# Block 2's low-rank gate row: both weight halves in one stationary tile, and its second layer in fp32r

## The reference, cut to what matters

```python
n = rms_norm(x, attn_norm_g)
proj = n @ w_in
(g_qkv, g_lr, g_out, nq, kc, vc, ks, vs, kw, vw, ng) = jnp.split(proj, offsets, axis=-1)
...
# gla_mixer: g_lr is 256 x 16, gate_w2 is 16 x 512
log_a = jax.nn.log_sigmoid((gate_lr @ gate_w2 + gate_b).astype(jnp.float32)) / GLA_GATE_TAU
...
# nsa_mixer: ng is 256 x 24
gates = jax.nn.sigmoid(gate_logits.astype(jnp.float32))
```

## Time and profile before

| what | value |
|---|---|
| median of 3 runs | 2610.11 us (2608.5 to 2611.57) |
| the profiled execution | 2613.08 us, span 2611.3 us |
| PE busy | 2594.8 us, 99% of the span |
| DVE, ACT, POOL busy | 43%, 54%, 46% |
| granted clock of PE, mean | 0.998 |
| transfers | 515.84 MB, 198 GB/s on average |

### The profile page before, as it was taken

The page is one execution under the profiler, slowest core; times in us unless marked ns, Lnnn a source line. Parts: engine busy times, 40 slices in busy tenths (PEclk is TensorE's granted clock), DMA queues, the critical chain, the costliest instruction groups (busy, mean ns, idle before and its releaser), DMA issues.

```text
span 2611.3 us, 30136 instructions
## 1 busy us (share of the span) xinstructions
PE 2594.8 (99%) x11856; PEld 2147.6 (82%) x11856; DVE 1130.2 (43%) x1328; ACT 1408.1 (54%) x1727; POOL 1205.6 (46%) x528
## 2 busy tenths in 40 slices
PE   8999999999999999999999999999999999999999
PEld 6888888788888888888888888878888888888887
DVE  5798955434342232323333466446533232322222
ACT  7667645445565555555544574565555555555333
POOL 2687843344444444444444455333344444444443
PEclk9999999999999999999999999999999999999999
DMA  8666654476566666666666644454666666666564
GB/s 299 214 193 202 191 194 164 148 234 210 191 204 205 208 202 209 202 209 202 209 206 213 208 162 161 160 195 139 184 202 201 209 201 209 202 209 202 201 201 145
DMA packets 174588, 515.84 MB, mean 198 GB/s; under 512 B 108027, under 2 KB 111068, under 8 KB 117104
## 3 DMA queue, kind: packets, MB, share of 16 engines
q1 hardware_dynamic: 174016, 513.40, 61.2%
q10 hardware_dynamic: 432, 0.52, 0.1%
HBM read 487.14 MB, written 2.10 MB: 187 GB/s over the span
## 4 chain that ended last, share of the span: by engine, by line
PE 95%; DVE 2%; ACT 1%; POOL 1%; issue 1%; DMA 0%; SPq 0%; ACTq 0%; DVEq 0%; POOLq 0%
PE PB L735 30%; PE PB L739 30%; PE PB L736 30%; DVE WL L2011 1%; ACT WH L1256 1%; POOL WL L2972 1%; PE PB L971 1%; PE PB L815 0%; PE PB L855 0%; PE PB L845 0%; PE PB L933 0%; PE PB L753 0%; PE PB L1088 0%; PE PB L917 0%; PE PB L1031 0%
## 5 line engine op out<-in xcount | busy, mean ns | idle before, releaser
L2972 POOL TENSOR_TENSOR WL<-RAW,WH 128x1024 fp32r<-128x1024 f32 x441 | 1084.4, 2459 | 1388.4 <-ACT WH L1256 1388.2
L1256 ACT ACTIVATE WH<-RAW 128x1024 fp32r<-128x1024 f32 x889 | 939.0, 1057 | 1078.6 <-PE PB L739 1060.2
L2011 DVE TENSOR_TENSOR WL<-RAW,WH 128x1024 fp32r<-128x1024 f32 x448 | 611.1, 1365 | 1391.1 <-ACT WH L1256 1390.9
L735 PE MATMUL PB<-WH,HNH 128*128 128x512 f32 x2464 | 970.8, 394 | 2.8 <-ACT WH L1544 2.1
L739 PE MATMUL PB<-WL,HNH 128*128 128x512 f32 x2464 | 962.0, 390 | 3.5 <-POOL WL L2972 3.4
L736 PE MATMUL PB<-WH,HNL 128*128 128x512 f32 x2464 | 960.6, 390 | 0.0
L739 PEld LDWEIGHTS PB<-WL,HNH 128*128 128x128 f32 x2464 | 463.3, 188 | 104.4 <-POOL WL L2972 6.3
L735 PEld LDWEIGHTS PB<-WH,HNH 128*128 128x128 f32 x2464 | 463.9, 188 | 102.5 <-issue 6.8
L736 PEld LDWEIGHTS PB<-WH,HNL 128*128 128x128 f32 x2464 | 463.7, 188 | 94.7
L735 PE MATMUL PB<-WH,HDH 128*128 128x512 f32 x704 | 273.9, 389 | 0.0
L736 PE MATMUL PB<-WH,HDL 128*128 128x512 f32 x704 | 273.9, 389 | 0.0
(11 more groups left out here) (377 smaller groups left out, 1930.4 us busy)
## 6 DMA issues: line engine op xcount, KB each, us to landing
RAW<-in_w_gu SPq DMA_DIRECT2D x176, 1024.0 KB, 4.8
RAW<-in_w_dn SPq DMA_DIRECT2D x88, 1024.0 KB, 4.8
RAW<-in_w_in_a SPq DMA_DIRECT2D x53, 1024.0 KB, 5.1
RAW<-in_w_in SPq DMA_DIRECT2D x45, 1024.0 KB, 4.8
RAW<-in_w_out SPq DMA_DIRECT2D x32, 1024.0 KB, 4.8
RAW<-in_w_ga SPq DMA_DIRECT2D x24, 1024.0 KB, 4.8
RAW<-in_w_gb SPq DMA_DIRECT2D x24, 1024.0 KB, 4.8
WIN<-in_win SPq DMA_DIRECT2D x8, 512.0 KB, 6.0
```

The source lines that it names most:

```text
L735: e.matmul(o, hi[:, k, x], WH[:, s, c], start=k == 0, stop=False)
L1256: e.activation(WH[:, u % NSPL, :], RAW[:, n % NRAW, half * SU * 128:(half + 1) * SU * 128], ACT.Copy).then_inc(*wt.act.mark(("wh", u)))
L2011: e.tensor_tensor(WL[:, u % NSPL, :], RAW[:, n % NRAW, half * SU * 128:(half + 1) * SU * 128], f32(WH[:, u % NSPL, :]), ALU.subtract).then ...
L2972: e.tensor_tensor(WL[:, u % NSPL, :], RAW[:, n % NRAW, half * SU * 128:(half + 1) * SU * 128], f32(WH[:, u % NSPL, :]), ALU.subtract).then ...
```

## The change

**The row.** The 40 columns are laid out in 64: `g_lr` (16), the first 16 of `ng`, `g_lr` again, the last 8 of `ng` with 8 of zeros; the 64 stand twice in the tile of 128. `WH` gets the rounded weights as before. The subtraction of the row's two units then writes the rest into the second 64 columns of `WH` itself (`low_of`), so that a stationary tile holds the high halves in its first 64 columns and the low halves in the others. Two products, with the high and with the low input, replace three. The wait for the low half stands ahead of a unit's first product.

**The second layer.** `GW2` is loaded as four stacked copies (128 x 512), each 16 rows and 16 of zeros. ACT rounds it to `GWR`, at step 3 of the row; DVE replaces the rows 32 to 47 and 96 to 111 by the low part, two operations at step 10. `LRS` is rounded to `LRH` by ACT (step 4 of `c1`) and its rest goes to `LRL` by DVE (step 7 of `c1`). Eight fp32r products with 128 rows replace four fp32 products with 16.

**The gates.** PE adds up high and low logits and turns them in one step, two fp32 products of `LRS` (stationary) with a table of ones, `gsel`, 24 columns wide, now in `c1` at tile 20. ACT takes the Sigmoid from PSUM at step 27 of `c1`; Sigmoid and copy on `GT` are gone.

```diff
+        def low_of(u):
+
+            n, half = divmod(u, 2)
+            raw, hi = RAW[:, n % NRAW, half * SU * 128:(half + 1) * SU * 128], WH[:, u % NSPL, :]
+            if u // 2 != both_halves // 2:
+                return WL[:, u % NSPL, :], raw, f32(hi)
+            raw, hi = (x.rearrange("p (t s c) -> p t s c", s=2, c=64)[:, :, 1, :] for x in (raw, hi))
+            return hi, raw, f32(hi)
...
                     if r == 0:
-                        e.wait_ge(*wt.act.done("wh", u))
+                        e.wait_ge(*low_half(u))
                     e.matmul(o, WH[:, s, c], hi[:, k, :], start=n == 0, stop=False)
-                    e.matmul(o, WH[:, s, c], lo[:, k, :], start=False, stop=False)
-                    if r == 0:
-                        e.wait_ge(*low_half(u))
-                    t = e.matmul(o, WL[:, s, c], hi[:, k, :], start=False, stop=last)
+                    t = e.matmul(o, WH[:, s, c], lo[:, k, :], start=False, stop=last)
...
             def decay_rows():
                 bz = [wide_bank("z", 0), wide_bank("z", 1)]
-                e.wait_ge(*m.act.done("lr"))
-                e.wait_ge(landed["gw2"], 16)
+                e.wait_ge(*m.act.done("lrh"))
+                e.wait_ge(*m.dve.done("gw"))
+                e.wait_ge(*m.dve.done("lrl"))
                 for h in range(4):
-                    t = e.matmul(bz[h // 2][:, (h % 2) * T:(h % 2 + 1) * T], GW2[:, h * 128:(h + 1) * 128], LR[:, :],
-                                 start=True, stop=True)
+                    z, w2 = bz[h // 2][:, (h % 2) * T:(h % 2 + 1) * T], GWR[:, h * 128:(h + 1) * 128]
+                    e.matmul(z, w2, LRH[:, :], start=True, stop=False)
+                    t = e.matmul(z, w2, LRL[:, :], start=False, stop=True)
...
             for k in tiles(16):
+                if k == 3:
+                    e.wait_ge(landed["gw2"], 16)
+                    e.wait_ge(*m.dve.done("lm"))
+                    e.activation(GWR[:, :], GW2[:, :], ACT.Copy).then_inc(*m.act.mark("gw"))
...
-                if k == 5:
+                if k == 4:
                     e.wait_ge(*m.dve.done("lr"))
-                    e.activation(LR[:, :], LRS[0:16, :], ACT.Copy).then_inc(*m.act.mark("lr"))
-                    e.activation(GT[32:56, :], LRS[32:56, :], ACT.Sigmoid).then_inc(*m.act.mark("gt"))
+                    e.activation(LRH[:, :], LRS[:, :], ACT.Copy).then_inc(*m.act.mark("lrh"))
+                if k == 27:
+                    e.wait_ge(*m.pe.done("gate"))
+                    e.activation(flat(GATE[:, :, :]), bank("gate")[:, 0:48], ACT.Sigmoid).then_inc(
+                        *m.act.mark("gate", frees("gate")))
...
+                if k == 10:
+                    e.wait_ge(*m.act.done("gw"))
+                    for p in (slice(32, 48), slice(96, 112)):
+                        e.tensor_tensor(GWR[p, :], GW2[p, :], f32(GWR[p, :]), ALU.subtract).then_inc(
+                            *m.dve.mark(*(["gw"] if p.start == 96 else [])))
...
+                if k == 7:
+                    e.wait_ge(*m.act.done("lrh"))
+                    e.tensor_tensor(LRL[:, :], LRS[:, :], f32(LRH[:, :]), ALU.subtract).then_inc(*m.dve.mark("lrl"))
```

More of the change, by code:

```diff
@@ L35, in vec_layout @@
                     ("qg", 1), ("kcg", 1), ("ksg", 1), ("kwg", 1),
-                    ("f1", 1), ("b1", 1), ("f2", 1), ("b2", 1), ("gbias", 1), ("gsum", 72)):
+                    ("f1", 1), ("b1", 1), ("f2", 1), ("b2", 1), ("gbias", 1), ("gsum", 72), ("gsel", 24)):
         VECS[name] = (n, k)
@@ L316, in build @@
         RST = ar("RST", [128, T], 47)
-        LR = ar("LR", [16, T], 38)
+        LRH = ar("LRH", [128, T], 38, F32R)
+        LRL = ar("LRL", [128, T], 39, F32R)
         LRS = ar("LRS", [128, T], 64)
-        GW2 = ar("GW2", [16, 512], 36)
+        GW2 = ar("GW2", [128, 512], 36)
+        GWR = ar("GWR", [128, 512], 32, F32R)
         MGH = ar("MGH", [128, 8, T], 48, F32R)
@@ L327, in build @@
         AM = ar("AM", [128, 384], 84)
-        GT = ar("GT", [56, T], 85.5)
         GATE = ar("GATE", [128, 2, 24], 86.5)
@@ L368, in build @@
         units = 2 * len(order)
+        both_halves = 2 * order.index(("w_in2", 4))
         def is_split(u):
@@ L1183, in gates_turned @@
                 bank = wide_bank("gate")
-                e.wait_ge(*m.act.done("gt"))
+                n = VECS["gsel"][0]
+                e.wait_ge(*m.dve.done("lr"))
                 for c in range(2):
-                    t = e.transpose(bank[:, c * 24:(c + 1) * 24], GT[32:56, c * 128:(c + 1) * 128], IDENT[32:56, 32:56])
+                    t = e.matmul(bank[:, c * 24:(c + 1) * 24], LRS[:, c * 128:(c + 1) * 128], VEC[:, n:n + 24],
+                                 start=True, stop=True)
                 t.then_inc(*m.pe.mark("gate"))
@@ L1190, in tensor @@
             tile_row(NT["lr"], 16, None, {2: lambda: scales_in_rows(2, ST), 8: lambda: turn_group("cg", 0)})
-            group(NT["c1"], HNH, HNL, 16, None, {16: decay_rows})
+            group(NT["c1"], HNH, HNL, 16, None, {16: decay_rows, 20: gates_turned})
             w.marks = second_marks(w.i)
@@ L1197, in tensor @@
                     group(NT["og"] + 2 * j, HNH, HNL, 16, None,
-                          {} if j else {8: lambda: turn_group("cg", 1), 32: gates_turned})
+                          {} if j else {8: lambda: turn_group("cg", 1)})
                 elif name == "v":
@@ L2008, in low @@
                     return
-                n, half = divmod(u, 2)
+                to, raw, hi = low_of(u)
                 e.wait_ge(*wt.act.done("wh", u))
-                e.tensor_tensor(WL[:, u % NSPL, :], RAW[:, n % NRAW, half * SU * 128:(half + 1) * SU * 128],
-                                f32(WH[:, u % NSPL, :]), ALU.subtract).then_inc(*wt.dve.mark(("wl", u)))
+                e.tensor_tensor(to, raw, hi, ALU.subtract).then_inc(*wt.dve.mark(("wl", u)))
             def tiles(n):
@@ L2589, in heads @@
                         if h == 0:
-                            e.wait_ge(*m.dve.done("gate"))
+                            e.wait_ge(*m.act.done("gate"))
                         for c in range(2):
@@ L2923, in vector @@
                             conv_earlier("cg", 1, (k - 14) // 4)
[L2924 to L2927, removed]
                     elif name == "v" and j or name == "kc":
@@ L2969, in low @@
                     return
-                n, half = divmod(u, 2)
+                to, raw, hi = low_of(u)
                 e.wait_ge(*wt.act.done("wh", u))
-                e.tensor_tensor(WL[:, u % NSPL, :], RAW[:, n % NRAW, half * SU * 128:(half + 1) * SU * 128],
-                                f32(WH[:, u % NSPL, :]), ALU.subtract).then_inc(*wt.pool.mark(("wl", u)))
+                e.tensor_tensor(to, raw, hi, ALU.subtract).then_inc(*wt.pool.mark(("wl", u)))
             def tiles(n):
@@ L3211 @@
         groups(w[:, 0:512]),
-        units(tiles(padded(np.concatenate([padded(w[:, 2048:2064], 32), w[:, 5648:5672]], axis=1)))),
+        units(tiles(np.concatenate([np.concatenate([w[:, 2048:2064], w[:, 5648:5664], w[:, 2048:2064],
+                                                    padded(w[:, 5664:5672], 16)], axis=1)] * 2, axis=1))),
         groups(w[:, 512:1024]), groups(w[:, 2064:3088]), groups(w[:, 1024:2048]), groups(w[:, 4112:4624]),
@@ L3226 @@
     a["filt_w3"] = np.ascontiguousarray(np.tile(one["filt_w3"].reshape(64, 2, 2, 1024), (2, 1, 1, 1)))
-    a["gla_gate_w2"] = np.ascontiguousarray(one["gla_gate_w2_2"])
+    a["gla_gate_w2"] = np.ascontiguousarray(np.tile(np.pad(one["gla_gate_w2_2"], ((0, 16), (0, 0))), (4, 1)))
     a["x"] = np.ascontiguousarray(x["x"][0].reshape(2, 128, 2048).transpose(1, 0, 2))
@@ L3264 @@
     put("gsum", apart.reshape(128, 72))
+    pick = np.zeros((64, 24), np.float32)
+    for i in range(24):
+        pick[16 + i if i < 16 else 32 + i, i] = 1.0
+    put("gsel", np.tile(pick, (2, 1)))
     put("gbias", one["mlstm_gate_bias"].reshape(16, 1))
```

## The result

| | before | after |
|---|---|---|
| median, runs side by side on one chip | 2611.57 us (2608.37 to 2614.07, 16 runs) | 2615.73 us (2612.14 to 2617.56, 16 runs) |
| ratio of the times | | 1.0018, 95% interval 1.0012 to 1.0025 |
| profiled execution | 2613.08 us, span 2611.3 us | 2616.26 us, span 2614.4 us |
| row's first product to PE's last product | 1496.53 to 2607.67, 1111.14 us | 1495.34 to 2610.83, 1115.49 us |

The account below looks back on a forecast made before the run. PE, busy 99% of the span, was taken as the bound. Chain +1.64, gates +0.15 and clock +1.6 gave +3.4 us on a median of 2610.11: 2613.5 us, range 2609.0 to 2615.5.

Parts of the forecast that it names:

- A wait of 4.5 us should do the same: After PE's wait at the second layer, the clock halves for 3.4 us, costing 1.6 us.
- the third rival: Behind the forecast wait at the second layer, half clock lasts 6.8 us: +5.0 us, 2615.1; chance 0.10.
- The chain, +1.64: Ahead of the second layer PE waits 4.5 us for LRL; c1 goes on 1.64 us later, instead of 2.88 earlier.
- The gates, +0.15: In c1, two fp32 products replacing two transposes take 0.45 us of PE instead of 0.30, a loss of 0.15.
- DVE gets in first: DVE's second GWR subtraction beats POOL; PE waits 2.3 us; -0.5 us, with or without the clock's 1.6; chance 0.22.
- No wait: LRL is ready when PE reaches the second layer; 2.7 us gained, 2607.4; chance 0.08.

Follow-up runs that it names:

- e7: Changed kernel plus one idle 128 x 512 copy on ACT, delaying a weight copy and POOL's subtraction behind it; 2612.55 us, ratio 1.0008 to before.
- e6: Changed kernel with the row put back to 48 products, leaving only the new second layer; 2610.41 us, ratio 0.9998 to before.
- e3: Changed kernel plus 20 thrown-away products on PE just ahead of its wait for LRL; 2613.62 us, ratio 1.0013 to before.
- e1: Changed kernel with PE's second layer moved from tile 16 to 32 of c1, gates from 20 to 28; 2612.86 us, ratio 1.0007 to before.
- b1: Changed kernel with GWR prepared in c0 and LRL ahead of the second conv_earlier on DVE; 2609.59 us, ratio 0.9995 to before.
- b2: Second visit of the same kernel as b1; 2609.19 us, ratio 0.9994 to before.
- e2: Changed kernel with GWR's copy and two subtractions moved earlier, into c0; 2610.18 us, ratio 0.9993 to before.
- e4: Changed kernel with LRL moved ahead of the second conv_earlier on DVE; 2613.29 us, ratio 1.0010 to before.

## Why the prediction missed

*What was right.* The order of events was as forecast at every link, in us behind the row's first product (forecast, measured): c1's first product 5.14, 5.12; GWR's copy 2.55, 2.54; C3's copy 5.47, 5.43; POOL's C3 6.59, 6.59; GWR's first subtraction 6.11, 6.23; conv_earlier 9.54, 9.76; LRS 12.06, 12.29; LRL 14.74, 14.96; the second layer 15.22, 15.53. POOL got in first, as forecast, with a lead of 0.35 us on the recorded start of the second subtraction; e7 shows that this order was the cause and e6 that it needs both halves of the change.

*The step that failed: "A wait of 4.5 us should do the same. Price: 3.4 x (1 - 0.23/0.43) = 1.6 us."* That the wait would be followed by half clock was right; the price of it was too low. I took the length of the half clock from one wait of 2.67 us in one trace. The change's wait of 4.78 us had 6.8 us at half clock, 1.7 of them in the wait and 5.11 under work. At the forecast's own rate 5.11 x (1 - 0.23/0.43) is 2.38, and e3 measures 2.36 in place of 1.6. The traced execution does not look like an odd one: over the change's 16 runs the mean granted clock is 0.9978, over the 85 runs of before beside the other kernels 0.9989, and a difference of 0.0011 over 2614 us is, as an estimate, 5.7 us at half clock. So the low stretch of the third rival, "half the clock for 6.8 us after it, as at the start", came true, without its price of 3.2, since 1.7 us of it fell into the wait.

My reason against that rival ("at 63.8, also dense, 3.4 us were enough") rested on a single execution, and so did the 3.4 itself. The wait of rows 9 stands in nine of the twelve traces, between 58 and 64 us and 2.60 to 2.71 us long. In six of them 3.4 us at 0.50 follow it or begin in it; in three (e1, e3 and e7) there is none. In e7, which loses 3.4 us to half clock behind its wait of 2.68 us at the second layer, the wait and the window behind it are
```profile
63.10 0.47 PE L812 MATMUL PB<-W3H,HS 128*128 128x512 f32 x1 [2.71 <-DVE W3L L2120]
```
```profile
63.10:66.50 3.40, 3.40 (x15) 2.84 (x16) 0.00 (x0) 0.78 (x1) 0.00 (x0) 1.00 0.94 246
```
Waits of one length thus came with half clock and without, and one row could not give the price. In the runs a longer wait went with a longer low stretch (6.8 us behind 4.78, 3.4 behind 2.68 and 3.01), but with one trace of each, that its length did this is not shown.

*The chain, +1.64.* It came out 0.31 late at the second layer's start, made of 0.12 at GWR's pair, 0.10 up to conv_earlier, and 0.09 between LRL and PE's first product.

*The gates, +0.15.* At full clock they cost about 0.04 net: in e6 c1 falls back by 0.45 us where the two fp32 products stand, and og gets 0.41 back where the transposes were.

Together: chain and gates 1.79 forecast, 1.99 measured in e3; clock 1.6 forecast, 2.36 measured; +3.4 against +4.35 in the traces, and +4.16 between the two medians. So 0.76 of the 2.2 us by which the median missed are the change's effect, mostly the clock's. The remainder is the baseline: I added +3.4 to a median of three runs, 2610.11, while before measured 2611.57 over the 16 runs beside the changed kernel, 1.46 higher. Either of the two put right alone would have moved the range past 2615.73, so that the time fell outside it took both. With the row's own start scattering over 5 us, three runs were too few to carry a range that ended 2 us above the forecast.

*The rivals.* "DVE gets in first" did not happen by itself, but e7 is it: forecast -0.5, or +1.1 with the clock's 1.6, and measured +1.58. "No wait" is b1 and b2: forecast -2.7, measured -2.80 and -2.63.

## What to carry to other kernels

When an operand is to be prepared by a chain over several engines, write out that chain against the time at which the shortened work will ask for it; here 2.9 us of saved products were worth nothing until the chain was moved, and then 2.6 to 2.8 by the traces. Price a wait of TensorE as the wait and the low clock behind it, and take that clock as a range from several traces: the same wait can come with it and without. A range around a median of three runs has to hold the scatter of that median as well.

## What the runs showed of the hardware

- Waits of PE of 0.76 (e6) and 1.11 us (e2) left the granted clock at 1.00; behind waits of 2.68 (e7) and 3.01 us (e4) came 3.4 us at 0.50, which cost 1.7 each; the wait of 4.78 had 6.8 us at 0.50 and cost 2.36, and filled with products that nobody uses it cost nothing in clock. One wait of 2.60 to 2.71 us near 60 us had 3.4 us at 0.50 in six traces and none in three.
- A POOL subtraction that comes 0.35 us ahead of a DVE one with two SBUF inputs costs DVE 2.1 us; 0.16 us behind it, DVE loses nothing and POOL 0.4. Adding an idle copy of 0.66 us to ACT therefore made the stretch from the row on 2.77 us shorter, 0.68 of it by the shorter half clock.
- Four fp32 products of 128 x 128 by 256 columns took 1.53 us, the same with a tile 16 rows deep 1.92; eight fp32r products of that size took 1.03 behind a wait (e6, 1508.33 to 1509.36) and 0.95 without one (b1).
